# Layout of the experts' weights on the partitions: neighbouring rows, 16 KB in one piece, in a retention and mixture-of-experts block

## What is computed

```python
hx2 = _modulate(_rmsnorm(x, norm2_w), shift, scale)          # [256, 1024]
g_logits = t @ rg_w + rg_b; e_logits = t @ re_w + re_b        # router, 4 groups x 8 experts
...                                                           # best group, its 2 best experts
for e in range(32):
    hid = t @ w13[e]                                          # [1024, 1024], 4 MB of f32
    act = jax.nn.silu(hid[:, :512]) * hid[:, 512:]            # gate half, up half
    out = out + combine[:, e:e + 1] * (act @ w2[e])           # [512, 1024], 2 MB of f32
```

## Time and profile before

| | |
|---|---|
| median of 3 runs | 1205.27 us (1200.65 to 1205.41) |
| profiled execution, span | 1207.0 us |
| busy over the span: TensorE, VectorE, ScalarE | 91%, 74%, 60% |
| HBM read | 294.92 MB |
| experts' chunks | 96 of 2 MB |

### The profile page before, as it was taken

The page is one execution under the profiler, slowest core; times in us unless marked ns, Lnnn a source line. Parts: engine busy times, 40 slices in busy tenths (PEclk is TensorE's granted clock), DMA queues, the critical chain, the costliest instruction groups (busy, mean ns, idle before and its releaser), DMA issues.

```text
span 1207.0 us, 16558 instructions
## 1 busy us (share of the span) xinstructions
PE 1099.4 (91%) x6355; PEld 932.1 (77%) x6355; DVE 891.4 (74%) x849; ACT 721.8 (60%) x688; POOL 17.5 (1%) x37
## 2 busy tenths in 40 slices
PE   2798999999999999997989999999999999999983
PEld 2396878888778899995678778787788877878772
DVE  3865355384365657557559998999999899999974
ACT  4733435353354433445258878887888788878762
POOL 1000000000000000001000000000000000000000
PEclk9898999999999999998589999999999999999996
DMA  9943126272344645546338999999999999999950
GB/s 330 329 141 140 70 93 256 71 256 94 140 164 160 236 145 204 190 176 204 138 140 299 345 348 335 354 360 352 345 355 361 355 334 359 345 364 330 363 214 37
DMA packets 126803, 296.70 MB, mean 246 GB/s; under 512 B 3068, under 2 KB 3292, under 8 KB 126756
## 3 DMA queue, kind: packets, MB, share of 16 engines
q1 hardware_dynamic: 125156, 292.66, 67.3%
q0 software_dynamic: 1600, 3.38, 1.0%
HBM read 294.92 MB, written 1.05 MB: 245 GB/s over the span
## 4 chain that ended last, share of the span: by engine, by line
PE 59%; DVE 12%; DMA 11%; issue 10%; ACT 8%; DVEq 1%; SPq 0%; ACTq 0%
DMA raw<-in_expert_w 10%; PE ps L507 8%; PE ps L508 8%; PE ps L509 8%; DVE lo L295 7%; ACT hi L288 6%; PE ps L519 3%; PE ps L520 3%; PE ps L521 3%; PE ps L728 3%; PE ps L729 3%; PE ps L749 3%; PE ps L707 2%; PE ps L627 2%; PE ps L770 2%
## 5 line engine op out<-in xcount | busy, mean ns | idle before, releaser
L295 DVE TENSOR_TENSOR lo<-raw,hi 128x2048 fp32r<-128x2048 f32 x276 | 619.9, 2288 | 125.6 <-ACT hi L288 124.1
L288 ACT ACTIVATE hi<-raw 128x2048 fp32r<-128x2048 f32 x276 | 517.4, 1917 | 179.4 <-PE ps L509 105.5
L728 PE MATMUL ps<-hi,xg 128*128 128x512 f32 x512 | 201.7, 394 | 3.6 <-DVE actp L1388 1.9
L729 PE MATMUL ps<-lo,xg 128*128 128x512 f32 x512 | 201.0, 393 | 0.0
L507 PE MATMUL ps<-hxh,hi 128*128 128x256 f32 x576 | 166.1, 288 | 5.8 <-DVE hxl L1121 4.5
L508 PE MATMUL ps<-hxl,hi 128*128 128x256 f32 x576 | 164.3, 285 | 0.0
L509 PE MATMUL ps<-hxh,lo 128*128 128x256 f32 x576 | 164.3, 285 | 0.0
L770 PE MATMUL ps<-hi,actp 128*128 128x512 f32 x256 | 107.9, 422 | 17.4 <-issue 13.7
L728 PEld LDWEIGHTS ps<-hi,xg 128*128 128x128 f32 x512 | 97.1, 190 | 26.2 <-issue 4.0
L507 PEld LDWEIGHTS ps<-hxh,hi 128*128 128x128 f32 x576 | 111.7, 194 | 6.8 <-issue 5.0
L729 PEld LDWEIGHTS ps<-lo,xg 128*128 128x128 f32 x512 | 97.1, 190 | 20.0
(11 more groups left out here) (246 smaller groups left out, 1492.9 us busy)
## 6 DMA issues: line engine op xcount, KB each, us to landing
raw<-in_expert_w SPq DMA_DIRECT2D x96, 2048.0 KB, 9.7
raw<-in_w_in SPq DMA_DIRECT2D x22, 2048.0 KB, 7.9
raw<-in_w_mod SPq DMA_DIRECT2D x12, 2048.0 KB, 9.6
raw<-in_w_ret_o SPq DMA_DIRECT2D x4, 2048.0 KB, 7.8
raw<-in_w_conv_o SPq DMA_DIRECT2D x2, 2048.0 KB, 8.2
raw<-in_w_out SPq DMA_DIRECT2D x2, 2048.0 KB, 8.5
xtok<-in_x SPq DMA_DIRECT2D x1, 1024.0 KB, 7.3
xtok<-in_ctx SPq DMA_DIRECT2D x1, 1024.0 KB, 10.4
```

Source lines behind the costliest of these rows:

```text
L288: eng.activation(hi[part_slot][:, k, :], raw[raw_slot][:, k, :], ACT.Copy).then_inc(hi_done, 1)
L295: eng.tensor_tensor(lo[part_slot][:, k, :], raw[raw_slot][:, k, :], hi[part_slot][:, k, :], ALU.subtract).then_inc(lo_done, 1)
L728: pe.matmul(ps[:, 4 + half, :], xg[:, s, k, :], hi[slot][:, k, :], start=(k == 0), stop=False)
L729: last = pe.matmul(ps[:, 4 + half, :], xg[:, s, k, :], lo[slot][:, k, :], start=False, stop=(k == 7))
```

## The change

Partition p now holds the features 8p to 8p+7 of w13 and the rows 4p to 4p+3 of w2. Each of the three chunks is then one piece of 16 KB for each partition. Chunk A is now the first four of a partition's eight rows with all 1024 columns, and chunk B the other four, so each holds a part of both the gate and the up half. The first product goes over A for both halves in turn (16 matmuls), then over B for the gate half (8 matmuls, then the new semaphore `gate_full`) and for the up half (8 matmuls, then `chunk_done`). What the weights meet is laid out alike: `hx2` is written with its features permuted, through a new buffer `xmod`, the router's weights are loaded in the same order, and `hs` is written permuted, so that the turn yields hidden features 4q+k for the partition q.

```diff
-        w13_v = expert_w13[0].rearrange("e (k p) n -> e p k n", p=P)
-        w2_v = expert_w2[0].rearrange("e (k p) n -> e p k n", p=P)
+        w13_v = expert_w13[0].rearrange("e (p k) n -> e p (k n)", k=KT)
+        w2_v = expert_w2[0].rearrange("e (p k) n -> e p (k n)", k=4)
...
-                    load(r, p13, w13_v[e][:, :, 0:512])
-                    load(r, nxt(p13), w13_v[e][:, :, 512:1024])
+                    load(r, p13, w13_v[e][:, 0:4 * D])
+                    load(r, nxt(p13), w13_v[e][:, 4 * D:8 * D])
...
-            pool.dma_start(rw[:, :, 0:NG], router_group_w[0].rearrange("(k p) n -> p k n", p=P)).then_inc(in_landed["router"], 16)
+            pool.dma_start(rw[:, :, 0:NG], router_group_w[0].rearrange("(p k) n -> p k n", k=KT)).then_inc(in_landed["router"], 16)
...
                 def first_product(i, s, n):
+
+                    def products(wh, wl, c, kk, half):
+                        k = 4 * c + kk
+                        col = slice(half * HID, (half + 1) * HID)
+                        pe.matmul(ps[:, 4 + half, :], xg[:, s, k, :], wh[:, kk, col], start=(k == 0), stop=False)
+                        return pe.matmul(ps[:, 4 + half, :], xg[:, s, k, :], wl[:, kk, col], start=False, stop=(k == 7))
...
+                    if not isinstance(n, int) or n > 0:
+                        pe.wait_ge(act_ready, n)
+                        pe.wait_ge(sel_ready, n)
+                        pe.wait_ge(cw_ready, n)
+                    for kk in range(4):
+                        if kk % 2 == 0:
+                            pe.wait_ge(lo_done, 2 * j + kk // 2 + 1)
+                        for half in range(2):
+                            last = products(wh, wl, 0, kk, half)
+                    last.then_inc(chunk_done, 1)
...
+                        for kk in range(4):
+                            if half == 0 and kk % 2 == 0:
+                                pe.wait_ge(lo_done, 2 * j + kk // 2 + 1)
+                            last = products(wh, wl, 1, kk, half)
+                        last.then_inc(gate_full if half == 0 else chunk_done, 1)
...
-                        act.wait_ge(chunk_done, number(r, first_half(i, s)) - C0 + half + 1)
+                        if half == 0:
+                            act.wait_ge(gate_full, n + 1)
+                        else:
+                            act.wait_ge(chunk_done, number(r, first_half(i, s)) - C0 + 2)
...
-                        act.activation(hs[:, half, :], ps[:, 4 + half, :], ACT.Copy).then_inc(hs_ready, 1)
+                        act.activation(hs[:, half, :].rearrange("p (k q) -> p q k", k=4),
+                                       ps[:, 4 + half, :].rearrange("p (q k) -> p q k", k=4), ACT.Copy).then_inc(hs_ready, 1)
...
-                        L(V.scalar_tensor_tensor(hx2[:, b, :], x1[:, b, :], stat[:, b:b + 1], scale2[:, :], ALU.mult, ALU.mult))
-                        V.tensor_tensor(hx2[:, b, :], hx2[:, b, :], shift2[:, :], ALU.add).then_inc(hx2_ready, 1)
+                        if b == 1:
+                            V.wait_ge(hx2_ready, 1)
+                        L(V.scalar_tensor_tensor(xmod[:, :], x1[:, b, :], stat[:, b:b + 1], scale2[:, :], ALU.mult, ALU.mult))
+                        V.tensor_tensor(hx2[:, b, :].rearrange("p (k q) -> p q k", k=KT), by_row(xmod), by_row(shift2),
+                                        ALU.add).then_inc(hx2_ready, 1)
```

More of the change, by code:

```diff
@@ L146, in block_kernel @@
         norm2 = at("norm2", 180, [P, D])
+        xmod = at("xmod", 180, [P, D])
         xg = at("xg", 160, [P, 2, KT, P], F32R)
@@ L226, in block_kernel @@
         p_ready, pw_ready, g_full, x_hi, x_lo = (sem(n) for n in ("p_ready", "pw_ready", "g_full", "x_hi", "x_lo"))
-        hs_ready, t_full, sa_ready, act_ready = (
-            sem(n) for n in ("hs_ready", "t_full", "sa_ready", "act_ready"))
+        gate_full, hs_ready, t_full, sa_ready, act_ready = (
+            sem(n) for n in ("gate_full", "hs_ready", "t_full", "sa_ready", "act_ready"))
         pt_full, sel_ready, cw_ready, y_full, y_hi, y_lo, s_done = (
@@ L392, in load @@
                 sp.wait_ge(lo_done, 2 * number(r, place) - 2 * RAW + 2)
-                wide_chunk = src.shape[1] == 4
-                sp.dma_start(wide(raw[slot]) if wide_chunk else raw[slot][:, :, :], src).then_inc(landed[slot], 16)
+                sp.dma_start(raw[slot][:, :, :].rearrange("p k n -> p (k n)"), src).then_inc(landed[slot], 16)
             def one_round(r):
@@ L711, in first_product @@
                 def first_product(i, s, n):
-                    place = first_half(i, s)
-                    for half in range(2):
[L714 to L724, removed]
-                        for k in range(8):
-                            if k % 4 == 0:
-                                pe.wait_ge(lo_done, 2 * j + k // 4 + 1)
-                            pe.matmul(ps[:, 4 + half, :], xg[:, s, k, :], hi[slot][:, k, :], start=(k == 0), stop=False)
-                            last = pe.matmul(ps[:, 4 + half, :], xg[:, s, k, :], lo[slot][:, k, :], start=False,
-                                             stop=(k == 7))
-                        last.then_inc(chunk_done, 1)
-                        place = nxt(place)
@@ new lines, in products @@
+                    def products(wh, wl, c, kk, half):
[3 more added lines that the diff above has]
+                        return pe.matmul(ps[:, 4 + half, :], xg[:, s, k, :], wl[:, kk, col], start=False, stop=(k == 7))
+                    place = first_half(i, s)
+                    j = number(r, place)
+                    wh, wl = wide(hi[place[1] % HLB]), wide(lo[place[1] % HLB])
@@ new lines, in first_product @@
+                    if s == 0:
+                        pe.wait_ge(x_hi, 2 * (g0 + i) + 2)
+                        pe.wait_ge(x_lo, 2 * (g0 + i) + 2)
+                    if not isinstance(n, int) or n > 0:
[7 more added lines that the diff above has]
+                            last = products(wh, wl, 0, kk, half)
@@ new lines, in first_product @@
+                    last.then_inc(chunk_done, 1)
+                    place = nxt(place)
+                    j = number(r, place)
+                    wh, wl = wide(hi[place[1] % HLB]), wide(lo[place[1] % HLB])
+                    for half in range(2):
+                        for kk in range(4):
[3 more added lines that the diff above has]
+                        last.then_inc(gate_full if half == 0 else chunk_done, 1)
@@ L1057, in done, with by_row @@
                 dve.wait_ge(dve_step, steps_done[0])
+            def by_row(t):
+                return t[:, :].rearrange("p (q k) -> p q k", k=KT)
             def quad(first):
```

2 lines of the change are left out of this document (1 added, 1 removed).

## The result

| | before | after |
|---|---|---|
| median of 4 runs | 1202.96 us (1197.38 to 1205.41) | 1235.18 us (1232.87 to 1237.40) |
| ratio, 95% interval | | 1.0265 (1.0224 to 1.0305) |
| span of the profiled execution | 1207.0 us | 1231.1 us |

The change makes the kernel slower by 2.65%. The profiled execution of before was longer than its four runs and that of after was the shortest of its own, so the two traces lie 24.1 us apart where the medians lie 32.2 apart.

The account below looks back on a forecast made before the run. DMA was taken to bound the experts at 35.95 us a pair. Head +3.6, first loaded pair -1.5, thirteen pairs -3.5, tail 0 and `hx2` +0.1 gave -1.3 us, so 1204 us, range 1193 to 1215.

Parts of the forecast that it names:

- late gate: ScalarE's gate copy in the even expert waits for 24 matmuls, not 16, and starts 1.25 us late.
- part 3: Small edits: strided `hs` writes cost nothing extra (upper bound 0.59 us more each); `hx2` adds 0.1 us.
- Rival 3: Strided `hs` copies on ScalarE cost double, +1.18 us, half of it per pair; 1217 us; chance 0.17.
- The halving: A delay in the even expert counts half per pair, since the way back and VectorE's run together span two pairs.
- part 2: Late gate copy in the even expert: 35.50 us a pair, 35.68 with 0.18 for the clock.
- two stretches: The way back and VectorE's run hand over to each other; their average gives 34.88 us a pair with free loads.
- The way back: TensorE and ScalarE, from `xg` to VectorE's lo of B in the next odd expert: 36.44 us, growing to 37.69.
- VectorE's run: VectorE's stretch from lo of B to the end of `xg`: 33.31 us, with no wait worth the name.
- part 1: Expert loads in 16 KB pieces run at 420 GB/s, 30 us a pair, so DMA drops out of the sum.
- DMA sets the pace: Among the experts a pair takes what its loads take: 12.58 MB at 350 GB/s, 35.95 us.
- Head and first loaded pair: First two experts: both first copies 1.8 us later, +3.6 us; first loaded pair 37.20 to 35.68 us, -1.5.
- The tail: Last even expert: late copy (+1.2 us) against a wait for a landing (about -1.0), taken as 0.

Follow-up runs that it names:

- e10: e5 plus four matmuls with unread results ahead of the even expert's turn; 1204.53 us, 1.0039 of before.
- e7: The changed kernel plus eight matmuls with unread results ahead of the even expert's turn; 1221.01 us, 1.0161 of before.
- e5: The changed kernel with w2 in its old layout (4 KB pieces) and `hs` copied and read in plain order; 1208.30 us, 1.0065 of before.
- e14: The changed kernel with the permuted copies of `hs` and `hx2` reading in steps and writing without gaps; 1208.74 us, 1.0058 of before.
- e1: The changed kernel with `hs` copied in plain order and the turn's transposes reading in steps of four elements; 1284.27 us, 1.0706 of before.
- e17: e16 plus eight matmuls with unread results ahead of the even expert's turn; 1213.10 us, 1.0102 of before.
- e16: The kernel before plus two useless ScalarE copies ahead of the even expert's second `hs` copy; 1225.72 us, 1.0187 of before.
- e13: The kernel before with only the experts' loads in 16 KB pieces, so its results differ from the reference's; 1196.44 us, 0.9966 of before.
- e3: The kernel before with A and B as row halves in 4 KB pieces, the new product order and late gate copy, nothing permuted; 1209.26 us, 1.0076.
- e15: e14 with hi of A(n+1) ahead of the gate copy on ScalarE; 1198.87 us, 0.9979 of before.
- e4: The changed kernel with hi of A(n+1) ahead of the gate copy on ScalarE; 1220.89 us, 1.0158 of before.
- e11: The kernel before plus four matmuls with unread results ahead of the even expert's turn; 1201.18 us, 0.9986 of before.

## Why the prediction was wrong

The forecast was 1204 us, no change, from 35.68 us a pair; measured are 37.66. The loss has three parts, which can be told apart in ratios to before: e10, which has the late gate but neither the strided `hs` copy nor a fall of the clock among the experts, stands at 1.0039; e7, with the strided copy and the full clock, at 1.0161; after, with both, at 1.0265. So the late gate costs some 0.4% net of what the pieces bring, the strided copies 1.2%, and the clock 1.0%. (w2 is in 4 KB pieces in e10 and in 16 KB pieces in e7; e5 and e14, which differ in the same way, are equal.) The traces say the same for a pair: 35.64 us in e5, e10 and e14 at full clock; 36.59 with the strided copies; 37.58 on the mean over all 14 loaded pairs of after, seven of them with a fall that adds 1.98. That is +0.95 and +0.99, 14 pairs of each, 13.3 and 13.9 us. The terms aren't independent: without the strided writes alone (e14) 26 us go, because most of the clock's loss goes with them.

**The strided writes of `hs`, taken at nothing** (part 3). This is the first failed step. I took the lower bound because the nearest row was the plain copy, though no row had the order in question. The copy went from 0.59 to 1.11 us, +0.52, near the upper bound of double; e14 shows that the order in which it goes is the cause, since the same permutation, read in steps from PSUM, costs nothing. Rival 3 had the mechanism, and the even expert's two copies as its carriers, but took half of them, 0.59 us a pair.

The Trainium skill ("SBUF — State Buffer", Specifications (TRN2)) says that an SBUF line has 16 bytes and that full bandwidth needs two hits in each. The traces agree wherever SBUF was stepped through by 16 bytes or more: 591 to 1108 ns for ScalarE's write, 1226 to 1906 for VectorE's write, 1998 for VectorE's reads, 194 to 327 for the weight loads of e1. I had set its warning against a missing price, and let the missing price win.

**The halving (part 2 and rival 3).** The second failed step. The copies' extra counts in full. It lies in the first of the three parts of a pair, from `xg` to the even expert's `sa`: 17.74 us in e10, 18.67 in after's short pair, while the other 17.91 us are the same. Two copies of +0.52 are 1.04, and 0.93 was found, in every pair. The odd expert's two copies add nothing to a pair: ScalarE's wait ahead of its `sa` shrinks instead, from 2.96 us in e10 to 2.32 in e7. The average of two stretches couldn't show this. The way back from an `xg` to lo of B in the next odd expert, and VectorE's run from lo of B to the next `xg`, add up to two pairs in any kernel with a steady loop, whatever holds it; halving a delay also assumes that VectorE's run stays at 33.31 us when the way back grows. It didn't: it is 33.72 in e10 (from 886.77 to 920.49) and 34.62 in e7 (898.17 to 932.79), since VectorE waits for `sa` and hi in it.

**The clock, taken at 0.18 us a pair** (part 2). I scaled what the clock had cost before. But the wait that my own working foretold, 1.3 to 1.6 us ahead of the even turn, became 2.15 us with the dear copies, and in every second pair the clock is down for 6.8 us behind it. That costs 1.98 us in the pair that it strikes, 0.99 on the mean. e7 shows it on after, e17 against e16 on before.

**The rate of the pieces, 420 GB/s** (part 1). It was 378 at full share (336 / 0.888 in after's 650 to 1150, the window below), 379 in e13. The line through two queue-alone rows held for 2 KB and 4 KB and was stretched to 16 KB. The price of the overstatement is small here, because with the late gate in place DMA dropped out of the sum at either rate:

```profile
q1 hardware_dynamic: 11535, 168.02, 88.8%
```

**"DMA sets the pace".** That 12.58 MB at 350 GB/s are 35.95 us says nothing: rate and time are of the same window, so the product must come out. The waits said 1.0 us an expert, and e13 answers directly: with loads 5% quicker, hi waits as long as ever, and the pair wins 0.55 us. Loads wait for a buffer that VectorE frees, so the landing is a link in a loop with hi and lo, and only part of it goes when the transfer gets quicker; that last point is argued from the queue's share of 93.6%, and no run with a fourth buffer tried it.

**What held.** 35.50 us were worked out for free loads with the late gate, and e5, e10 and e14 found 35.64. The number is in part luck. In the nearly free pair of before, between its `xg` rows at 887.11 and 922.04, `sa` and the next lo are these:

```profile
903.53 0.39 ACT L1000 ACTIVATE sa<-ps 128x256 f32<-128x256 f32 x1 [2.09 <-PE ps L749]
...
906.84 4.49 DVE L295 TENSOR_TENSOR lo<-raw,hi 128x2048 fp32r<-128x2048 f32 x2
```

That is 16.42 + 3.31 + 15.20 us, and e10 has 17.74 + 2.86 + 15.05, so that 1.32 were lost in the first part and 0.60 won in the rest, where VectorE had been the later one. (That pair was not quite free: ScalarE waited 2.29 us in it for a landing, of which 0.17 reached VectorE, whose four halves of lo took 9.06 us instead of 8.89.) That slack is used up once, and the copies' extra came on top in full.

ScalarE waited for the gate half, 1.18 us on the mean (15.4 / 13) where 1.25 was worked out. Waits for landings vanished (1.2 us in 500). DMA's share fell to 0.88. The pitch of 32 KB did no harm that shows: the rate in it was the highest; no run changed the pitch alone. Head and first loaded pair were given +3.6 and -1.5, together +2.1; from the start of the first product to the end of that pair the traces have +4.5, in part by the strided writes, which I hadn't counted there. The two sums of `hx2` took 1.4 us more, not 0.1. The tail, taken at 0, gave -0.9.

**Where the pieces' gain went.** Pieces alone are worth 0.34% (e13). In after they are lost at once: the late gate takes their gain and more (e10 is 0.39% over before at full clock; e3 and e5 are equal), and the strided copies and the clock come on top. With the late copy covered by hi of A(n+1) and the permutation on the reading side, the change comes to 0.9979 (e15), which can't be told from before.

Open stays why the clock falls in every second pair and not in each, though the wait is the same length in all of them; how much of e4's 14 us is the wait itself and how much the clock; and whether the step or the short innermost loop makes ScalarE's write dear.

## What to carry to other kernels

A permuted copy is a term of the sum: price it by the step in SBUF, and if the source is in PSUM, let the reading side step and the writing side run without gaps. A delay counts by half only while the engine that it hands over to has slack; look which parts of the loop stay constant from run to run before halving it. A new wait of TensorE must be priced with the clock that it may cost; a few useless matmuls put into the wait are a cheap experiment that tells the two apart, if the trace afterwards shows that the falls are gone (they weren't in e11). And a rate times a time from the same window doesn't show what sets the pace; change the rate alone, as e13 did, before believing that the loads do.

## What the runs showed of the hardware

- ScalarE, 128x512 of f32 from PSUM into SBUF: 591 ns in order, 1108 ns with successive elements 512 bytes apart, 590 ns when the step of 16 bytes is on the PSUM side (after, e14).
- VectorE, 128x1024 of f32 in SBUF: 1226 ns in order (before), 1906 ns with the output written in steps of 512 bytes (after), 1998 ns with both inputs read in steps of 32 bytes (e14).
- TensorE, weight load 128x128 of f32: 194 ns in order (before), 327 ns in steps of 16 bytes (e1).
- A kernel became faster by 14 us through 8 x 15 matmuls that nobody needs, since the clock stayed at 2.4 GHz in all loaded pairs (e7); in after it fell to 1.2 GHz for 6.8 us in every 75.1 us, always behind the wait of 2.15 us ahead of the even turn. In e11 it fell four times with waits of 1.4 us at another place.
- Among the experts, rate divided by share is 378 GB/s for pieces of 16 KB, 360 for 2 and 4 KB mixed, and 172.80 MB / 500 us / 0.936 = 369 for 4 KB alone (e3).
